# Overflow expert blocks of 32 slots, four to an array pass: four overflow passes per layer in place of five

## The reference: what is computed

```python
def hier_moe(xn, w_rg, b_rg, w_re, b_re, w_gate, w_up, w_down):
    ...
    p_g, g_idx = lax.top_k(gp, 1)                  # one of 4 groups
    ...
    tv, ti = lax.top_k(ep, TOP_K_FINE)             # two of the group's 4 experts
    ...
    h = jax.nn.silu(jnp.einsum('nd,edf->nef', xf, w_gate)) * jnp.einsum('nd,edf->nef', xf, w_up)
    y = jnp.einsum('nef,efd->nd', h * gates[:, :, None].astype(h.dtype), w_down)
```

## Time and profile before

| what | value |
|---|---|
| median of 3 runs | 3329.57 us (3328.66 to 3330.66) |
| the profiled execution, its own time | 3329.99 us |
| its span, first to last instruction | 3328.2 us |
| PE busy | 2948.6 us, 89% of the span |
| mean granted TensorE clock | 0.919 |
| moved from and to HBM | 673.04 MB read, 196.82 MB written |
| passes of layer 0, first product to last | 720.43 us to 1033.04 us |
| passes of layer 1, first product to last | 2947.70 us to 3259.94 us |

### The profile page before, as it was taken

The page is one execution under the profiler, slowest core; times in us unless marked ns, Lnnn a source line. Parts: engine busy times, 40 slices in busy tenths (PEclk is TensorE's granted clock), DMA queues, the critical chain, the costliest instruction groups (busy, mean ns, idle before and its releaser), DMA issues. The chain is left out here.

```text
span 3328.2 us, 35350 instructions
## 1 busy us (share of the span) xinstructions
PE 2948.6 (89%) x13465; PEld 1682.1 (51%) x13465; DVE 992.7 (30%) x2132; ACT 495.9 (15%) x868; POOL 89.3 (3%) x148
## 2 busy tenths in 40 slices
PE   6999998979995999999978869987996996979995
PEld 4676766633332677676752254445445443533333
DVE  1202131021112232210045564446456443221113
ACT  2012110021111111001021121121112110021113
POOL 0000000000000000000000000000000000000000
PEclk9999968989996999999988779987997998989997
DMA  3333415189995533343319918955991995388994
GB/s 120 111 117 103 152 44 191 27 322 370 351 384 218 185 116 99 97 137 117 123 44 404 413 66 328 405 199 187 402 382 50 368 408 210 136 317 353 375 389 148
DMA packets 287073, 745.95 MB, mean 224 GB/s; under 512 B 45440, under 2 KB 89052, under 8 KB 277700
## 3 DMA queue, kind: packets, MB, share of 16 engines
q1 hardware_dynamic: 273756, 673.85, 54.7%
q0 software_dynamic: 8960, 65.02, 4.9%
q10 hardware_dynamic: 4224, 5.24, 0.4%
HBM read 673.04 MB, written 196.82 MB: 261 GB/s over the span
## 5 line engine op out<-in xcount | busy, mean ns | idle before, releaser
L2406 DVE SCALAR_TENSOR_TENSOR ring<-ring,small,psum 128x512 f32<-128x512 f32 x512 | 355.7, 744 | 409.5 <-PE psum L2340 408.7
L1127 PE MATMUL psum<-x_norm,ring 128*128 128x320 f32 x1280 | 350.3, 436 | 4.0 <-DVE x_norm L286 4.0
L1127 PEld LDWEIGHTS psum<-x_norm,ring 128*128 128x128 f32 x1280 | 245.3, 192 | 107.9 <-issue 8.4
L1755 PE MATMUL psum<-x_norm,ring 128*128 128x320 f32 x1024 | 279.2, 435 | 6.1 <-DMA ring<-in_l_w_up 6.1
L353 PE MATMUL psum<-x_norm,ring 128*128 128x320 f32 x1024 | 278.7, 436 | 4.0 <-DVE x_norm L286 4.0
L1755 PEld LDWEIGHTS psum<-x_norm,ring 128*128 128x128 f32 x1024 | 195.5, 191 | 88.4 <-DMA ring<-in_l_w_up 6.6
L353 PEld LDWEIGHTS psum<-x_norm,ring 128*128 128x128 f32 x1024 | 196.2, 192 | 86.5 <-issue 6.4
L353 PE MATMUL psum<-arena,ring 128*128 128x320 f32 x768 | 210.3, 437 | 14.7 <-DMA ring<-in_l_w_down 8.4
L2340 PE MATMUL psum<-ring 72*128 72x512 bf16 x512 | 182.1, 406 | 31.7 <-DVE ring L2406 22.5
L2329 PE MATMUL psum<-ring,x_norm 128*32 128x256 f32 x2048 | 173.2, 412 | 29.3 <-DMA ring<-in_state_mlstm_C 28.7
L686 PE MATMUL psum<-ring,x_norm 128*64 128x512 f32 x896 | 197.0, 595 | 0.0
(11 more groups left out here) (418 smaller groups left out, 2785.0 us busy)
## 6 DMA issues: line engine op xcount, KB each, us to landing
ring<-in_state_mlstm_C SPq DMA_DIRECT2D x256, 512.0 KB, 8.0
out_s_m_C<-ring SPq DMA_DIRECT2D x256, 512.0 KB, 6.8
ring<-in_l_w_up SPq DMA_DIRECT2D x64, 1024.0 KB, 5.2
ring<-in_moe_w_gate SPq DMA_DIRECT2D x112, 512.0 KB
ring<-in_moe_w_up SPq DMA_DIRECT2D x112, 512.0 KB
arena<-in_moe_w_down SPq DMA_DIRECT2D x112, 512.0 KB
arena<-in_moe_w_gate SPq DMA_DIRECT2D x96, 512.0 KB
arena<-in_moe_w_up SPq DMA_DIRECT2D x96, 512.0 KB
```

Of the source, the lines that this page charges most:

```text
L1127: mm = pe.matmul(m.psum[:, t, 0:T], slots[:, s, k, t * P:(t + 1) * P], m.XN[:, KPS * s + k, :], start=(s == 0 and k == 0), stop=(s == SLOT ...
L1755: mm = pe.matmul(m.psum[:, t, 0:T], slots[:, s, k, t * P:(t + 1) * P], m.XN[:, KPS * s + k, :], start=(s == 0 and k == 0), stop=(s == SLOT ...
L2406: dve.scalar_tensor_tensor(part_c, part_c, wcol[:, h, bass.ds(b, 1)], m.psum[:, 5 + e, :], ALU.mult, ALU.add).then_inc(updated, 1)
```

## The change

Overflow blocks hold 32 slots (`PART`) in place of 64, and 16 of them are reserved in place of 10. Four overflow blocks, with four experts' weights, share a pass of 128 slots: each takes 32 columns of the array. So there are four overflow passes (8 to 11) and 12 passes in all. An overflow pass has 16 gate and up units and 8 down units, a regular one 8 and 4 as before. The ring keeps its 16 units, and SP's rule for waiting is the same. The tables that find a row's block are made for units of 32 slots.

```diff
 CAP = 64
-OVER = 10
-PAIRS = NE // 2 + OVER // 2
+PART = 32
+OVER = 16
+PAIRS = NE // 2 + OVER // 4
+PARTS = PAIRS * P // PART
 UNITS = 16
-ORDER = (0, 1, 8, 2, 9, 3, 10, 4, 11, 5, 12, 6, 7)
+ORDER = (0, 1, 8, 2, 9, 3, 4, 10, 5, 11, 6, 7)
...
-    def gate_up_unit(p):
-        return 8 + 12 * (p - 1) if p else 0
-
-    def down_unit(p):
-        return 16 + 12 * p if p < PAIRS - 1 else 8 + 12 * p
+    parts = [2 if o < NE // 2 else 4 for o in ORDER]
+    gate_up_unit, down_unit, n = [], [], 0
+    for p in range(PAIRS):
+        gate_up_unit.append(n)
+        n += 4 * parts[p]
+        if p:
+            down_unit.append(n)
+            n += 2 * parts[p - 1]
+    down_unit.append(n)
...
-                units = [gate_up_unit(p) + 2 * s + i for i in range(2)]
+                w = P // parts[p]
+                units = [gate_up_unit[p] + parts[p] * s + i for i in range(parts[p])]
                 for u in units:
                     pe.wait_ge(landed[u % UNITS], 32 * (u // UNITS + 1))
                 for c in range(4):
                     for i, u in enumerate(units):
-                        w = slots[u % UNITS].rearrange("p a (c f) -> p a c f", c=4)
-                        mm = pe.matmul(m.psum[64 * i:64 * i + 64, 0, :], x_t[:, 4 * s + c, 64 * i:64 * i + 64], w[:, :, c, :],
+                        weights = slots[u % UNITS].rearrange("p a (c f) -> p a c f", c=4)
+                        mm = pe.matmul(m.psum[w * i:w * i + w, 0, :], x_t[:, 4 * s + c, w * i:w * i + w], weights[:, :, c, :],
                                        start=(s == 0 and c == 0), stop=(s == 3 and c == 3))
...
-            for i in range(2):
-                for q in range(6):
-                    n = TILES[q % 3][1]
-                    mm = pe.matmul(m.psum[64 * i:64 * i + 64, 7, 0:PAIRS], rank_hot[0:n, q, :], in_block[0:n, q, i:26:2],
-                                   start=(q == 0), stop=(q == 5))
+            for q in range(6):
+                n = TILES[q % 3][1]
+                for i in range(4):
+                    mm = pe.matmul(m.psum[PART * i:PART * i + PART, 7, 0:PAIRS], rank_hot[0:n, q, :],
+                                   in_block[0:n, q, i:PARTS:4], start=(q == 0), stop=(q == 5))
...
-            for q in range(2, T // CAP):
+            for q in range(1, (T - CAP) // PART):
                 dve.drain()
-                dve.scalar_tensor_tensor(spare, total, float(CAP * q), spare, ALU.is_gt, ALU.add)
+                dve.scalar_tensor_tensor(spare, total, float(CAP + PART * q), spare, ALU.is_gt, ALU.add)
```

More of the change, by code:

```diff
@@ L238, in _ @@
             dve.tensor_scalar(m.route[:, 0:NE], m.route[:, 0:NE], float(CAP), -float(CAP + 1), ALU.mult, ALU.add)
-            rank_in, first, token = (m.route[:, a:a + n] for a, n in ((42, CAP), (42 + CAP, 27), (69 + CAP, 3)))
-            dve.tensor_tensor_scan(rank_in, m.ones[:, 0:CAP], m.ones[:, 0:CAP], 0.0, ALU.mult, ALU.add)
-            dve.tensor_tensor_scan(first, m.ones[:, 0:27], m.ones[:, 0:27], 0.0, ALU.mult, ALU.add)
+            rank_in, first, token = route_tables(m)
+            dve.tensor_tensor_scan(rank_in, m.ones[:, 0:PART], m.ones[:, 0:PART], 0.0, ALU.mult, ALU.add)
+            dve.tensor_tensor_scan(first, m.ones[:, 0:PARTS + 1], m.ones[:, 0:PARTS + 1], 0.0, ALU.mult, ALU.add)
             dve.tensor_reduce(token[:, 0:1], m.causal[:, :], AX_X, ALU.add)
@@ L508, in moe @@
     slot_i = view(m.small, 744, 2, 3).bitcast(I32)
[L509 to L513, removed]
+    below = view(m.xn, 4096, OVER, NE)
+    over_f = view(m.small, 752, OVER)
+    over_e = view(m.small, 768, OVER).bitcast(I32)
+    over_on = view(m.small, 784, OVER).bitcast(I32)
+    on_f = view(m.small, 800, OVER)
     gate = view(m.small, 960, 2, 3)
     gate_parts = view(m.small, 968, 2, 3, 4)
[L516 to L520, removed]
+    from_block = view(m.arena, 16704, 6, PARTS + 1)
+    in_block = view(m.arena, 17024, 6, PARTS)
+    block_no = view(m.arena, 17320, 6)
+    rank_no = view(m.arena, 17328, 6)
+    rank_hot = view(m.arena, 17344, 6, PART)
+    rank_in, first_slot, token = route_tables(m)
     source = view(m.small, 996, PAIRS).bitcast(I32)
@@ L700, in project_down @@
             pe.wait_ge(hid_kept, p + 1)
-            units = [down_unit(p) + i for i in range(4)]
+            w = P // parts[p]
+            units = [down_unit[p] + i for i in range(2 * parts[p])]
             for u in units:
@@ L710, in project_down @@
                 for k in range(2):
-                    for i in range(2):
-                        w = slots[units[2 * k + i] % UNITS].rearrange("p a b -> p (a b)")
-                        mm = pe.matmul(m.psum[64 * i:64 * i + 64, 4 + n, :], hid_t[:, k, 64 * i:64 * i + 64],
-                                       w[:, n * 512:(n + 1) * 512], start=(k == 0), stop=(k == 1))
+                    for i in range(parts[p]):
+                        weights = slots[units[parts[p] * k + i] % UNITS].rearrange("p a b -> p (a b)")
+                        mm = pe.matmul(m.psum[w * i:w * i + w, 4 + n, :], hid_t[:, k, w * i:w * i + w],
+                                       weights[:, n * 512:(n + 1) * 512], start=(k == 0), stop=(k == 1))
                         if n == 3:
@@ L804, in keep_y @@
                     else:
-                        act.wait_ge(consumed, down_unit(p) + 4)
+                        act.wait_ge(consumed, down_unit[p] + 2 * parts[p])
                     if p and n == 2:
```

38 lines of the change are left out of this document (20 added, 18 removed).

## The result

The changed kernel takes 3397.76 us (median of 4, 3396.97 to 3401.54) against 3330.11 us for the kernel before beside it (3328.66 to 3330.93): a ratio of 1.0211, with a 95% interval of 1.0199 to 1.0224. It is 2.1% slower. The forecast was 3368 us with a range up to 3395, and the measured time lies 2.8 us above that range: the sign and the mechanism were right, the size was a little over half of what came (38 us of 68).

What follows compares the result with a forecast made beforehand. PE was taken to bound the passes, with DMA close behind. Passes 18.2 and 19.2 us longer plus 1.4 ahead of them gave 38.8 us on 3329.99, said as 3368 us; range 3346 to 3395, 8 in 10.

Steps and rivals of the forecast that it cites:

- the time of the loads once the ring opens: Behind an overflow pass's first group: down units flow from S + 5.25 at 0.412 MB per us, 2.55 us a unit.
- S: Start of an overflow pass's gate_up on PE, from which the forecast's schedule counts its times in us.
- Landing: From a load's last byte to PE's start: 1.0 us taken, where two rows of before gave 2.7 and 0.7.
- An overflow pass costs PE what it did: Overflow passes on PE: twice the products at 32 columns, four strips overlapping, the new pass counted at the same 23.43 us.
- The ring shuts, and PE waits 40 to 55 us per layer: Overflow pass's 16 empty units fill the ring, delaying later loads; PE waits 40 to 55 us per layer, before 5.6.
- The sum of the passes, +18.2 and +19.2 us: All passes of layers 0 and 1 together: 18.2 and 19.2 us longer than before, 37.4 in all.
- The clock, 2.1 us once per layer: Products behind a wait over 5 us run slower on PE: 2.1 us, counted once per layer.
- the rival that every wait chills the clock: Four waits per layer ahead of a last group each cost 2.1 us: 17 us more, 3385 us; chance 0.14.
- The tail, two regular passes at the end: After pass 11, with no more gathers: last project_down ends at S + 89.9, down units wait 6.3 us.
- The cancelling rival: Stalls and saving cancel if gathers and stores (17.9 us per layer) take no time from the weights: 3332 us; chance 0.06.
- The chain ahead of the passes: Table work ahead of the passes: list kept 2.4 us later, partly covered, so 1.4 us, all in layer 0.

Runs made afterwards that it cites:

- the filler runs: Unread products on resident data while PE waits: in the changed kernel 3393.76 us; in it with gathers and stores cut to two rows or postponed, 3413.94 us.

## Why the prediction was right in its sign and half its size

The step that failed is the time of the loads once the ring opens: the forecast had the full rate of 412 GB/s from S + 5.25 and 1.0 us from the last byte to PE's start, and the runs show 325 to 364 GB/s in the first ten microseconds and 2.4 us. With the gathers and stores taken out of both, forecast and kernel still differ by some 14 of the 16.1 us in layer 0 (under *Landing*). The rest is a gather that the tail put at nothing.

- *An overflow pass costs PE what it did.* Right: four strips overlap, 128 records in 13.95 us.
- *The ring shuts, and PE waits 40 to 55 us per layer.* Right: 46.0 and 43.2, down units issued at S + 3.66 (forecast about 3.5), DMA idle longer. Runs without overflow units and with 14 units show the mechanism, not only the symptom.
- *The sum of the passes, +18.2 and +19.2 us.* Wrong: +34.3 in both. By cycles of layer 0 (from one overflow `gate_up` to the next, or to the end), forecast and measured: 55.15 and 59.41, 89.6 and 91.87, 55.15 and 58.52, 89.9 and 96.05; together 16.1 us too short. The waits agree with the forecast only because part of the lateness hides elsewhere. Products of 64 columns took 67.1 + 51.0 + 43.6 + 25.2 = 186.9 us, and 168.7 in the run without overflow units: 18.2 us more, at the low clock. Waits and slow products, 64.2 us, are the loss of 65.0. The forecast had some 50 and 2.1.
- *The clock, 2.1 us once per layer.* The count was wrong: slow products stand behind nearly every wait of 2.7 us and more (9.32 us for 7.04, 5.26 for 3.65; from 804 to 806 us the granted clock is 0.50, the 1.2 of 2.4 GHz). But their price on the path is small: keeping the clock up won 1.0 to 1.6 us per layer, with the gathers or without, and up to 1.7 more if the last down products are counted. So the rival that every wait chills the clock had the rows right, but its price is not what was missing. The Trainium skill, "TensorE: Matmul & The Clock Gate", section "HAM oscillation — how this bites in real kernels", counts each cold start behind a DMA wait as lost; here the trace agrees with the cold start, and the filler runs show that the loads bind and the cold products fill time in which PE would otherwise have waited.
- *The tail, two regular passes at the end "with no more gathers".* Wrong, and the cycle with the largest miss: 96.05 us for 89.9. POOL's timeline around and after the start of the last overflow pass at 969.08:

```profile
967.49 0.57 POOL L655 DMA_DIRECT2D y_slots<-arena  x1 [26.33 <-ACT arena L823]
968.37 0.96 POOL L642 DMA_INDIRECT x_norm<-x_rows,small  x1 [0.30 <-issue]
997.73 0.57 POOL L655 DMA_DIRECT2D y_slots<-arena  x1 [28.40 <-ACT arena L823]
998.61 0.96 POOL L642 DMA_INDIRECT arena<-x_rows,small  x1 [0.30 <-issue]
1024.95 0.57 POOL L655 DMA_DIRECT2D y_slots<-arena  x1 [25.38 <-ACT arena L823]
```

PE at the second last down units:

```profile
1047.19 9.88 PE L728 MATMUL psum<-arena 128*64 128x512 f32 x32 [6.63 <-DMA arena<-in_moe_w_down]
```

  POOL asks for a gather only behind the store of three passes before, so the last gather goes out at S + 29.5, among the loads. My schedule has two stores there, 2.6 us each (in S + 39.5 and again in S + 72.7), and no gather. The second last down units reach PE at S + 78.1 instead of S + 72.7. Without the transfers the tail is 7.9 us shorter, 2.7 more than the 5.2 that I had; with the gathers asked for one pass earlier it is 2.8 shorter (93.26 us). The other 3.5 us of its miss are late loads.
- *Landing, 1.0 us from the last byte to PE's start, and loads from S + 5.25 at full rate.* This step failed: mis-sized. Of the 2.7 and 0.7 us that its own rows gave, the forecast took 1.0. In the first cycle DMA goes idle at about 801.4 (293 GB/s over the 2 us from 800), which is S + 42.1 where I had S + 41.0, after ten microseconds at 325 GB/s; PE starts 2.4 us later, not 1.0; and the next products follow 5.19 us behind for 3.45. 1.1, 1.4 and 1.7 make up the 4.3 us by which this cycle is longer than forecast, but for rounding. The other three cycles with one regular pass miss by 3.3 to 4.1 (58.43 to 59.26). It isn't the gathers and stores. With its terms for them taken out (5.1, 10.2, 5.1 and 5.2), the forecast's four cycles are 50.05, 79.4, 50.05 and 84.7 us; the run without them took 54.4, 82.0, 54.0 and 88.2, 14.3 more in layer 0 and 11.0 more in layer 1. The filler in that run won 1.1 and 1.6 us of this. So most of it is the loads; a run that changes their rate or their landing alone was not made. The Trainium skill, "DMA: Bandwidth & Descriptors", section "Anatomy of one DMA — SWDGE (gpsimd) path", puts most of a fixed 2.0 us between the last byte and the semaphore, for the other kind of queue; the 2.4 us here agree with it in size.
- *The cancelling rival's price of gathers and stores, 17.9 us.* The rival added up its own schedule wrongly: that counts 5.1 twice in the cycle with two regular passes and 2.6 twice in the tail, 25.6 us in all. Taken out, gathers and stores give 27.3 us, by cycle 5.0, 9.9, 4.5 and 7.9. So they cost about what their bytes cost, and the schedule lacked only the tail's gather. Even so the passes stay 6.9 and 4.0 us above those of before with its gathers in place, where the rival had 0.3 and 1.3.
- *The chain ahead of the passes, +1.4 us.* It doesn't decide. The count products, which I had at 1.0 us more, became 2.2 us shorter, four strips side by side, and the wait of PE for the tables ahead of them 1.4 longer, against the earlier trace rows:

```profile
701.53 1.21 PE L765 MATMUL psum<-arena 128*32 128x12 f32 x48 [7.45 <-DVEq L929]
```

## What to carry to other kernels

Count a prefetch ring in the places that stand between two real loads, not in bytes: an empty or skipped load holds its place until the consumer has passed it, and two places less cost 26 to 28 us per layer here. Where such a ring shuts and opens, size the stall from every byte that must pass while DMA is full, gathers and stores too, and do not take the idle time of the waiting engine as the whole loss, since a lower clock turns part of it into slow work. Before paying to keep the clock up, ask whether the loads would be in any earlier.

## What the hardware showed that I had not expected

A left-out conditional transfer is answered within about 0.2 us while real ones fill the DMA engines, but the engine that issues it was held for 3.4 us by two real transfers ahead of it; the same units on another engine's queue took the passes from 351.4 to 309.2 us. After an idle spell the weights came at 360 GB/s for the first 10 us, even with next to nothing else in the queues (share 0.98 to 1.02), where the rate later is 403 to 419; behind the other three overflow passes of that layer it was 351 to 387. In the run without gathers and stores:

```profile
765.00:770.00 5.00, 5.00 (x52) 1.52 (x48) 0.00 (x0) 0.00 (x0) 0.00 (x0) 1.00 0.98 360
770.00:775.00 5.00, 3.10 (x32) 0.69 (x24) 0.42 (x1) 0.39 (x1) 0.00 (x0) 1.00 1.02 364
775.00:780.00 5.00, 2.16 (x6) 0.85 (x8) 0.00 (x0) 0.00 (x0) 0.00 (x0) 0.59 1.03 419
```

It is not that down units come first: SP issued nothing but down units from 987.48 on in the kernel before, and DMA brought 411 and 410 GB/s from 1010 to 1020. What it is was not tried.
